# Second perceptron projection as seven half-size products per quarter of the inner width

## The reference

```
hm = rms_norm(x, norm_mlp) @ mlp_w1
x  = x + square(relu(hm)) @ mlp_w2
```

## Time and profile before

| | |
|---|---|
| device time, median of 3 runs | 1789.66 us (1789.11 to 1792.14) |
| profiled execution: span from first to last instruction | 1786.1 us |
| PE busy | 1751.6 us, 98% of the span, 9182 matmuls |
| POOL busy | 1101.4 us, 62% |
| DVE busy | 935.4 us, 52% |
| ACT busy | 474.9 us, 27% |
| chain that ended last | PE 91%, DVE 6% |

### The profile page before, as it was taken

One profiled execution on the slowest core, in us unless ns is written; L12 is line 12 of the kernel. 1 busy time (PEld: TensorE's weight loads), 2 busy tenths in 40 slices (PEclk: granted clock), 3 DMA queues, 4 the chain that ended last, 5 costly groups with the idle time before them and its releaser, 6 DMA issues.

```text
span 1786.1 us, 26166 instructions
## 1 busy us (share of the span) xinstructions
PE 1751.6 (98%) x9182; PEld 1466.1 (82%) x9182; DVE 935.4 (52%) x1537; ACT 474.9 (27%) x963; POOL 1101.4 (62%) x844
## 2 busy tenths in 40 slices
PE   6999999999999999999999999998999999999998
PEld 4888888888988888888888778886788778888887
DVE  4754727465455455554553698797466463213311
ACT  4121221211222223222321226644442522002200
POOL 3657555689754545554447658975055688667863
PEclk9999999999999999999999999999999999999999
DMA  9523222285423223322323332201032333333331
GB/s 353 175 86 95 76 82 76 83 323 165 141 85 87 76 68 93 91 78 67 90 77 95 95 88 59 72 18 43 1 118 59 90 99 98 102 94 94 94 101 52
DMA packets 282163, 176.00 MB, mean 99 GB/s; under 512 B 6064, under 2 KB 272624, under 8 KB 280816
## 3 DMA queue, kind: packets, MB, share of 16 engines
q1 hardware_dynamic: 275024, 151.01, 28.7%
q10 hardware_dynamic: 7072, 24.07, 3.7%
HBM read 172.31 MB, written 2.62 MB: 98 GB/s over the span
## 4 chain that ended last, share of the span: by engine, by line
PE 91%; DVE 6%; SPq 1%; DMA 1%; ACT 0%; issue 0%; ACTq 0%; DVEq 0%
PE acc L405 14%; PE acc L407 14%; PE acc L406 14%; PE ob L405 4%; PE ob L407 4%; PE ob L406 4%; PE acc L435 3%; PE acc L437 3%; PE acc L436 3%; PE sc L1710 2%; PE acc L453 2%; PE acc L454 2%; PE acc L455 2%; SPq L713 1%; PE sc L1615 1%; PE ob L1722 1%
## 5 line engine op out<-in xcount | busy, mean ns | idle before, releaser
L805 POOL TENSOR_TENSOR wl<-raw,wh 128x512 fp32r<-128x512 f32 x456 | 639.3, 1422 | 19.3
L802 POOL TENSOR_SCALAR wh<-raw 128x1024 fp32r<-128x1024 f32 (+1 forms) x232 | 272.6, 1175 | 567.3 <-PE acc L407 138.3
L405 PE MATMUL acc<-hh,wh 128*128 128x512 f32 x800 | 325.0, 406 | 1.4 <-ACT sq L1485 1.2
L407 PE MATMUL acc<-hh,wl 128*128 128x512 f32 x800 | 313.3, 392 | 0.0
L406 PE MATMUL acc<-hl,wh 128*128 128x512 f32 x800 | 312.7, 391 | 0.0
L405 PEld LDWEIGHTS acc<-hh,wh 128*128 128x128 f32 x800 | 151.1, 189 | 35.7 <-issue 2.7
L407 PEld LDWEIGHTS acc<-hh,wl 128*128 128x128 f32 x800 | 150.7, 188 | 32.8
L406 PEld LDWEIGHTS acc<-hl,wh 128*128 128x128 f32 x800 | 151.1, 189 | 32.1 <-issue 2.4
L405 PE MATMUL ob<-Yh,wh 128*128 128x512 f32 x256 | 100.6, 393 | 0.0
L407 PE MATMUL ob<-Yh,wl 128*128 128x512 f32 x256 | 99.8, 390 | 0.0
L406 PE MATMUL ob<-Yl,wh 128*128 128x512 f32 x256 | 99.7, 390 | 0.0
(11 more groups left out here) (575 smaller groups left out, 3706.3 us busy)
## 6 DMA issues: line engine op xcount, KB each, us to landing
raw<-in_att_w_in SPq DMA_DIRECT2D x64, 512.0 KB, 3.9
raw<-in_mlp_w SPq DMA_DIRECT2D x64, 512.0 KB, 3.8
raw<-in_ret_w_in SPq DMA_DIRECT2D x48, 512.0 KB, 3.7
ada_w<-in_ada_w ACTq DMA_DIRECT2D x8, 1536.0 KB, 7.2
raw<-in_w_in SPq DMA_DIRECT2D x23, 512.0 KB, 3.6
ada_w<-in_ada_w SPq DMA_DIRECT2D x16, 512.0 KB, 9.1
raw<-in_ret_w_out SPq DMA_DIRECT2D x16, 512.0 KB, 4.1
raw<-in_att_w_out SPq DMA_DIRECT2D x16, 512.0 KB, 4.0
```

The source lines that it names most:

```text
L405: e.matmul(bank[:, :], wh[:, s, k, :], rhs_high(k), start=(start and k == 0), stop=False)
L407: last = e.matmul(bank[:, :], wl[:, s, k, :], rhs_high(k), start=False, stop=(stop and k == k1 - 1))
L802: e.tensor_scalar(wh[:, s, 0:k1, :], raw[:, s, 0:k1, :], 1.0, 1.0, ALU.mult, ALU.mult).then_inc(high_done, 1)
L805: low = e.tensor_tensor(wl[:, s, k0:k0 + KT // 2, :], raw[:, s, k0:k0 + KT // 2, :], wh[:, s, k0:k0 + KT // 2, :].bitcast(F32), ALU.subtract)
```

## The change

W2's part of the perceptron is done by quarters of the inner width instead of halves: for each quarter 8 units of W1 and then, in place of 16 output half-tiles, one 512 x 1024 by 1024 x 1024 product by Winograd's form of Strassen's method. The activations of the quarter are a 2 x 2 arrangement A11, A12, A21, A22 (256 tokens by 512 inner features each), the weights B11, B12, B21, B22 (512 x 512 each). Seven products of half the size in each dimension replace eight: A11 B11, S1 T1, S2 T2, A22 T4, S4 B22, S3 T3, A12 B21, with sums S1 to S4 of activation blocks and T1 to T4 of weight blocks. Products are accumulated in three PSUM chains of two banks (U, V, W), and read out into x at places given in `READS`.

The output is now by tokens: the stationary operand is a 128 x 128 block of the activations, the moving one 512 columns of weights. So x itself is turned to tokens during the first quarter (`tokens_turned`, `token_out`), the norm is a per-partition scalar (`fneg` for the negative reads), no scale tile is spread, and the turning at the end is gone. The last product is done token tile by token tile, and eight DMAs of 256 KB write the result.

Who does what: POOL splits the W1 units as before and makes the weight sums T (`block_sum`, two subtractions of 128 x 512 for each of two halves of four sums); the high parts of all W2 operands are ACT copies of 128 x 1024 (`weights_high`) and their low parts DVE subtractions of 128 x 1024 (`weights_low`), 14 of each a quarter. For the activations DVE squares (`squared`), makes the sums (`combos`) and the low parts (`combos_low`), and ACT relu and the high parts (`combos_high`). W2 is loaded in blocks of 1 MB.

```diff
+OPERANDS = {"A11": 0, "S3": 1, "A12": 2, "A22": 3, "S1": 4, "S2": 5, "S4": 6}
+
+
+PRODUCT = [("A11", "B11", "U", True), ("S1", "B11", "V", True), ("S2", "B11", "U", False), ("A22", "B11", "W", True),
+           ("S4", "B22", "V", False), ("S3", "B12", "U", False), ("A12", "B21", "W", True)]
+READS = [[("U", 0, 0, 1)], [("V", 1, 1, 1)], [("U", 0, 1, 1)], [("W", 1, 0, -1)],
+         [("V", 0, 1, 1)], [("U", 1, 0, 1), ("U", 1, 1, 1)], [("W", 0, 0, 1)]]
+
+
+SUMS = [("T1", "B11", "B12", "B11"), ("T2", "B11", "B22", "B11"), ("T4", "B11", "B11", "B21"), ("T3", "B12", "B22", "B12")]
+SUM_OF = {1: "T1", 2: "T2", 3: "T4", 5: "T3"}
+BLOCKS = {"B11": 0, "B12": 1, "B21": 2, "B22": 3}
+PER = IN_UNITS + 2 * PRODUCTS
...
+        ych = at("mlp_high", [P, 7, 4, 2 * P], 0, F32R)
+        ycl = at("mlp_low", [P, 7, 4, 2 * P], 28 * KB, F32R)
+        blocks = at("mlp_blocks", [P, 4, 4, S], 56 * KB)
+        ykeep = at("mlp_kept", [P, 4, 3, 2 * P], 96 * KB)
+        ygroup = [at("mlp_group0", [P, 5, 2 * P], 88 * KB), sb("mlp_group1", [P, 5, 2 * P])]
...
+        CHAIN = {"U": ob, "V": sc, "W": [st, bc]}
...
+        def slot_used(m):
+
+            if m < 0:
+                return unit_used, total_units + m + 1
+            q, r = divmod(m, PER)
+            if r < IN_UNITS:
+                return PE.at(f"fi{q}{r}")
+            return PE.at(f"fp{q}{(r - IN_UNITS) // 2}{(r - IN_UNITS) % 2}")
+
+        def in_slot(q, j):
+            return (PER * q + j) % RING
+
+        def product_slot(q, i, h):
+            return (PER * q + IN_UNITS + 2 * i + h) % RING
...
+            load_in(0, range(RING))
+            load_in(0, (4, 5))
+            e.wait_ge(*V.at("nfss"))
+            load_block(0, "B11")
+            load_in(0, (6, 7))
+            load_block(0, "B12")
+            load_in(1, range(RING))
+            load_block(0, "B22")
+            load_block(0, "B21")
+            for q in range(1, QUARTERS):
+                e.wait_ge(*V.at(f"w_lo{q - 1}31"))
+                load_block(q, "B11")
+                e.wait_ge(*V.at(f"w_lo{q - 1}41"))
+                e.wait_ge(*G.at(f"T3{q - 1}1"))
+                load_block(q, "B22")
+                e.wait_ge(*V.at(f"w_lo{q - 1}51"))
+                load_block(q, "B12")
+                e.wait_ge(*V.at(f"w_lo{q - 1}61"))
+                load_block(q, "B21")
+                load_in(q, range(RING, IN_UNITS))
+                if q + 1 < QUARTERS:
+                    load_in(q + 1, range(RING))
...
+            def split_in(q, j):
+                n, s = q * IN_UNITS + j, in_slot(q, j)
+                x = raw[:, n % RING, :, :]
+                e.wait_ge(raw_full[n % RING], (total_units + n) // RING * 16 + 16)
+                e.wait_ge(*slot_used(PER * q + j - RING))
+                e.tensor_scalar(wh[:, s, :, :], x, 1.0, 1.0, ALU.mult, ALU.mult).then_inc(*G.done(f"f_hi{q}{j}"))
+                e.wait_ge(*G.at(f"f_hi{q}{j}"))
+                for k0 in (0, KT // 2):
+                    low = e.tensor_tensor(wl[:, s, k0:k0 + KT // 2, :], x[:, k0:k0 + KT // 2, :],
+                                          wh[:, s, k0:k0 + KT // 2, :].bitcast(F32), ALU.subtract)
+                low.then_inc(*G.done(f"f_lo{q}{j}"))
+
+            def block_sum(q, name, dst, a, b, h):
+                before = {"T1": 0, "T2": 1, "T4": 2}
+                if name in before:
+                    e.wait_ge(*V.at(f"w_lo{q}{before[name]}{h}"))
+                for x in (a, b):
+                    e.wait_ge(block_in[x], 16 * q + 16)
+                e.wait_ge(*G.last())
+                for c in range(2):
+                    o, x, y = (block_half(n, h)[:, c * S:(c + 1) * S] for n in (dst, a, b))
+                    last = e.tensor_tensor(o, x, y, ALU.subtract)
+                last.then_inc(*G.done(f"{name}{q}{h}"))
+
+            for q in range(QUARTERS):
+                for j in range(IN_UNITS):
+                    split_in(q, j)
+                for name, dst, a, b in SUMS:
+                    for h in range(2):
+                        block_sum(q, name, dst, a, b, h)
...
+            def token_out(k):
+                e.wait_ge(*PE.at(f"x_turned{k}"))
+                e.activation(xT[:, k, :], ob[k % 2][:, :], ACT.Copy).then_inc(*AC.done(f"x_tokens{k}"))
+
+            def relu(q, j):
+                e.wait_ge(*PE.at(f"fi{q}{j}"))
+                if q or j >= 6:
+                    e.wait_ge(*V.at(f"y_lo{q if j >= 6 else q - 1}{j + 4 if j < 4 else j + 2 if j < 6 else j - 2}"))
+                e.activation(y_pair(j), acc[j % 2][:, :].rearrange("p (a n) -> p a n", a=2), ACT.Relu)\
+                 .then_inc(*AC.done(f"y_relu{q}{j}"))
+
+            def combos_high(q, j):
+                e.wait_ge(*V.at(f"y_sum{q}{j}"))
+                src, dst = ((ykeep[:, j, 0:2, :], ych[:, 0:2, j, :]) if j < 4 else
+                            (ygroup[j % 2][:, :, :], ych[:, 2:7, j - 4, :]))
+                e.activation(dst, src, ACT.Copy).then_inc(*AC.done(f"y_hi{q}{j}"))
+
+            def weights_high(q, i, h):
+                of = PRODUCT[i][1]
+                e.wait_ge(*(G.at(f"{SUM_OF[i]}{q}{h}") if i in SUM_OF else (block_in[of], 16 * q + 16)))
+                e.wait_ge(*slot_used(PER * q + IN_UNITS + 2 * i + h - RING))
+                e.activation(flat(wh[:, product_slot(q, i, h), :, :]), block_half(of, h), ACT.Copy)\
+                 .then_inc(*AC.done(f"w_hi{q}{i}{h}"))
+
+            for q in range(QUARTERS):
+                for j in range(IN_UNITS):
+                    if q == 0:
+                        token_out(j)
+                    relu(q, j)
+                    combos_high(q, j)
+                    if j >= 4:
+                        weights_high(q, (j - 4) // 2, (j - 4) % 2)
+                for i in range(PRODUCTS - 2):
+                    for h in range(2):
+                        weights_high(q, i + 2, h)
...
+            def tokens_turned(k):
+                e.wait_ge(*AC.at(f"nfsq{k}"))
                 if k >= 2:
...
+            def product_free(q, i):
+                chain = PRODUCT[i][2]
+                before = [n for n in range(i) if PRODUCT[n][2] == chain]
+                if before or q:
+                    n = before[-1] if before else max(n for n in range(PRODUCTS) if PRODUCT[n][2] == chain)
+                    return V.at(f"x_read{q if before else q - 1}{n}")
+                return {"U": AC.at(f"x_tokens{KT - 1}"), "V": V.at("nfroot"), "W": V.at("nfroot")}[chain]
+
+            def product_block(q, i, k, t):
+                of, _, chain, start = PRODUCT[i]
+                s, c = product_slot(q, i, k // 2), OPERANDS[of]
+                high, low = (x[:, c, k, t * P:(t + 1) * P] for x in (ych, ycl))
+                bank, n = CHAIN[chain][t][:, :], 4 * (k % 2)
+                w, v = flat(wh[:, s, n:n + 4, :]), flat(wl[:, s, n:n + 4, :])
+                e.matmul(bank, high, w, start=(start and k == 0), stop=False, skip_group_check=True)
+                e.matmul(bank, low, w, start=False, stop=False, skip_group_check=True)
+                return e.matmul(bank, high, v, start=False, stop=(k == 3), skip_group_check=True)
+
+            def product_quarter(q, i):
+                e.wait_ge(*product_free(q, i))
+                by_token = q == QUARTERS - 1 and i == PRODUCTS - 1
+                for h in range(2):
+                    e.wait_ge(*V.at(f"w_lo{q}{i}{h}"))
+                    if by_token:
+                        continue
+                    for k in (2 * h, 2 * h + 1):
+                        if i == 0:
+                            e.wait_ge(*V.at(f"y_lo{q}{k}"))
+                        if i == 1:
+                            e.wait_ge(*V.at(f"y_lo{q}{4 + k}"))
+                        for t in range(2):
+                            last = product_block(q, i, k, t)
+                    last.then_inc(*PE.done(f"fp{q}{i}{h}"))
+                if by_token:
+                    for t in range(2):
+                        for k in range(4):
+                            last = product_block(q, i, k, t)
+                        last.then_inc(*PE.done(f"last{t}"))
...
+                    if q == 0 and j:
+                        if j == 2:
+                            e.wait_ge(*V.at("nfss"))
+                            columns(e, dg, 0, "first", "last", "nfcols")
+                        tokens_turned(j - 1)
+                        if j == IN_UNITS - 1:
+                            tokens_turned(j)
+                for i in range(PRODUCTS):
+                    product_quarter(q, i)
...
+            def squared(q, j):
+                o = y_pair(j)
+                e.wait_ge(*AC.at(f"y_relu{q}{j}"))
+                e.tensor_tensor(o, o, o, ALU.mult).then_inc(*V.done(f"y_raw{q}{j}"))
+
+            def combos(q, j):
+                e.wait_ge(*V.at(f"y_raw{q}{j}"))
+                if j < 4:
+                    e.tensor_tensor(ykeep[:, j, 1, :], ykeep[:, j, 0, :], ykeep[:, j, 2, :], ALU.subtract)\
```

(89 more changed lines are left out.)

144 lines of the change are left out of this document (36 added, 108 removed).

## The result

The changed kernel takes 1826.53 us (median of 4 runs, 1822.95 to 1826.63) against 1790.89 us before on the same chip: a ratio of 1.0199, 95% interval 1.0182 to 1.0216. It is slower by some 36 us. The forecast was 1828.

A forecast was written before the change was run, and what follows sets the result against it. PE's matmul starts, 0.227 us apart, were taken to bound the perceptron. Span 1786.1 less 24.4 won plus 63.1 of stalls gave 1824.8, plus 3.6 to the median 1828 us; range 1804 to 1843, its own 1817 to 1838.

The forecast's parts named there:

- What is removed: Perceptron and its end: four units less (21.8 us), spread norm gone, shorter end, slightly dearer turning; 24.4 us won.
- The turning: First quarter: PE waits for ACT's token copies and relu in units 2 to 7 and before product 0; 17.5 us.
- The ladder: Last W1 unit to product 2: chain of waits across ACT, DVE, POOL; 7.0 us a quarter, 5.2 in the first.
- the port: DVE instructions with two SBUF inputs and POOL's wait for each other; 5.0 us in three quarters, 3.0 in the first.
- nine meetings at 0.335: DVE and POOL meeting at their shared port in the ladder, about nine instructions at a mean 0.335 us each.
- upper bound of 9.4 us a quarter: Most the port could cost: 15 instructions a quarter at 0.63 us; the exclusive-lock rule would put the sum toward it.
- The clock: Rival: the clock falls while PE idles 5 to 8 us; 1860 us and more, chance 0.04.
- 0.2 to start again: PE after a wait: 0.2 us to restart, added to the waits in the turning and before product 2.
- The step from span to median: Whole kernel: the runs' median lies 3.6 us over the profiled span, taking 1824.8 to 1828 us.
- The faster rival: Product 2 isn't late, ladder under 10.9 us, only the turning's stalls remain; 1783 us, chance 0.11.

The follow-up runs named there:

- e9_square_from_psum: e8_early_weights with VectorE's square reading x from PSUM as second operand, the bank freed by it instead of by relu: 1770.57 us, 0.991 of the kernel before.
- e3_relu_first: Changed kernel with ScalarE's relu ahead of the token copies and turned tiles in the banks of chain V instead of U: 1816.59 us.
- e1_no_sums: Changed kernel without GpSimd's weight sums T1 to T4, every product taking the plain block (output not the reference's): 1790.85 us.
- e2_scratch_sums: Changed kernel with the weight sums still made but written to an unread scratch tile, products taking plain blocks: 1809.2 us.
- the fillers: Changed kernel with unused 512-column matmuls put ahead of TensorE's known waits: 1819.14 us.
- e5_streams: e3_relu_first plus A12 B21 second, A22 T4 last; on VectorE sums ahead of low parts, additions between weight parts: 1784.33 us, 0.9976 of the kernel before.
- e8_early_weights: e5_streams with the four weight parts of products 0 and 1 one unit earlier on ScalarE and VectorE: 1775.09 us, 0.9924 of the kernel before.

## Why the prediction was right, step by step

*What is removed.* Four units, 21.8 us: PE has 9082 matmuls instead of 9182 (96 of the products, 4 of the spread norm), and the spacing in the products is 0.227 us where the clock is full. The end: last matmul at 1817.35, end of the span 1821.1, 3.8 us as forecast, against 5.9. From the first perceptron matmul to the end of the span, the kernel before takes 1786.1 - 1425.4 = 360.7 us and e9_square_from_psum, which has almost no waits, 1767.6 - 1425.1 = 342.5. So 18.2 of the 24.4 us to be won are really won there; of the other 6.2, 4.9 are the waits that are left and about 1 the starts after them. The 24.4 us were there; what they took back is the rest of this section.

*The turning.* Forecast 17.5 us. In the trace product 0 starts 64.1 us after the first matmul, where 47.5 are work (eight units, turning and columns): 16.6 us late, 14.5 of them waits. The reading was right in place and kind. At 1434.90 ACT copies a token tile, 1435.39 it does the relu that had been ready, and PE goes on at 1436.13:

```profile
1434.27 0.60 PE L2489 MATMUL ob<-const,xT 128*128 128x128 f32 x4
1436.13 0.47 PE L2478 MATMUL acc<-hh,wh 128*128 128x512 f32 x1 [1.27 <-ACT mlp_kept L1570]
```

e3_relu_first then shows what I had not put in the sum: with these waits gone, 4.4 us come back before product 1. There VectorE's weight part for it starts at 1485.45, takes 1.22 and is ready at 1486.67, and PE goes on at 1486.77, while ScalarE's last token copy was done at 1482.28. The waits had covered that rung too.

*The ladder.* This is the main term. Forecast: product 2 starts 12.4 us late in three quarters and 8.4 in the first. Measured: product 0 of the second quarter at 1579.47, product 2 at 1600.71, 21.2 us where 10.9 are work: 10.3 late, the same in the other two, and 7.4 in the first (1487.47 to 1505.71). Together 38.4 against 45.6. The rungs, from ACT's, DVE's and POOL's timelines:

```profile
1581.89 0.58 ACT L1570 ACTIVATE mlp_group<-acc 128x512 f32<-128x512 f32 x1
...
1596.44 1.06 ACT L1583 ACTIVATE wh<-mlp_blocks 128x1024 fp32r<-128x1024 f32 x1 [3.66 <-POOL mlp_blocks L965]
```
```profile
1582.50 1.54 DVE L3381 TENSOR_TENSOR mlp_group<-mlp_group 128x512 f32<-128x512 f32 x1 [1.63 <-ACT mlp_group L1570]
1583.96 1.48 DVE L3397 TENSOR_TENSOR mlp_low<-mlp_group,mlp_high 128x1280 fp32r<-128x1280 f32 x1
1585.37 0.41 DVE L3390 TENSOR_TENSOR mlp_group<-mlp_kept,mlp_group 128x256 f32<-128x256 f32 x1
1585.81 0.42 DVE L3391 TENSOR_TENSOR mlp_group<-mlp_group,mlp_kept 128x256 f32<-128x256 f32 x1
...
1588.03 2.53 DVE L3397 TENSOR_TENSOR mlp_low<-mlp_group,mlp_high 128x1280 fp32r<-128x1280 f32 x1 [0.20 <-ACT mlp_high L1577]
1590.49 3.55 DVE L3403 TENSOR_TENSOR wl<-mlp_blocks,wh 128x1024 fp32r<-128x1024 f32 x2
1597.53 1.41 DVE L3403 TENSOR_TENSOR wl<-mlp_blocks,wh 128x1024 fp32r<-128x1024 f32 x1 [3.50 <-ACT wh L1583]
1599.05 1.61 DVE L3419 SCALAR_TENSOR_TENSOR xT<-ob,rs,xT 128x512 f32<-128x512 f32 x2
```
```profile
1592.86 3.56 POOL L965 TENSOR_TENSOR mlp_blocks<-mlp_blocks 128x512 f32<-128x512 f32 x2 [1.16 <-DVE wl L3403]
```

Each rung is where it was put, but the sizes were not. Relu 7 starts 2.4 us after product 0. The forecast has the same 2.4 (0.25 and 2.2 late) without the port, and 2.0 more for six meetings at the port in a turn of the cycle, together 4.4. In e1_no_sums relu 7 starts 1.6 us after product 0 (1578.33 and 1576.75). So the cycle alone was 0.8 us too long in the sum, and GpSimd's sums add 0.8 to it and not 2.0. From relu 7 on, dependent sums on DVE start 0.03 us after one another (1585.37 + 0.41 to 1585.81); I had taken 0.15 from an instruction with PSUM operands. And the meetings at the port in this ladder are 1.54 - 0.69 = 0.85 for the squares, 2.53 - 1.49 = 1.0 for the low parts, 3.55 - 2.35 = 1.2 for the two weight parts, 3.56 - 2.54 = 1.0 for T2, 0.2 for the last weight part: 4.3 us where nine meetings at 0.335 had been put at 3.0. With the 0.8 of the cycle the port comes to 5.1 us, against 5.0 in the sum. That this total fits is luck: five meetings at 0.86 on average in the ladder, not nine at 0.335. The 17.6 us between e1_no_sums and e2_scratch_sums fit the forecast's 18.0 for the port in the same way. Of the 2.1 us by which the ladder was too long in each of three quarters, 0.8 are the cycle, 0.4 the dependent sums and 0.6 the starts after waits, which don't delay product 2's start; 0.3 stay open.

What a meeting costs is the rest of the other engine's instruction. Low parts 7 start at 1588.03, beside a subtraction of GpSimd's that started first; GpSimd's next one runs until 1591.69, and VectorE's weight part ends 1.09 us behind it, at 1592.78:

```profile
1587.91 1.31 POOL L965 TENSOR_TENSOR mlp_blocks<-mlp_blocks 128x512 f32<-128x512 f32 x1 [4.42 <-DVE wl L3403]
1589.16 2.53 POOL L965 TENSOR_TENSOR mlp_blocks<-mlp_blocks 128x512 f32<-128x512 f32 x1
```
```profile
1590.49 2.29 DVE L3403 TENSOR_TENSOR wl<-mlp_blocks,wh 128x1024 fp32r<-128x1024 f32 x1
```

The Trainium skill, SBUF — State Buffer, "SBUF: two separate sides", states that a VectorE instruction with two SBUF inputs and a GpSimd instruction that reads SBUF lock the shared pair of ports against each other, for the whole instruction of the one that starts first. The traces agree: these three lines, and the square in e9_square_from_psum, 688 ns with one SBUF input where the means with two were 890 and 1225. The forecast had read from this rule that the sum would lie toward its upper bound of 9.4 us a quarter. It did not (5.1), because fewer instructions met than the fifteen counted, not because a meeting was cheap.

*The clock.* Here the forecast failed. I gave it as a rival with a chance of 0.04 and 1860 us, all or nothing, and the sum has nothing for it. It fell in every quarter, in short pieces, 65 slow matmuls. The step that was wrong is "0.2 to start again": after a wait the trace has 0.1 us more where the clock holds (0.34 to the next start, as at 1592.83) and 0.4 more where it is half (0.6 at 1600.71), followed by 5 to 13 slow matmuls. Behind product 2 this came to 3.0, 1.7, 2.6 and 1.5 us in the four quarters, 8.8 us, of which the fillers took away 8.4.

*The total.* Turning 16.6, ladder 38.4 and clock 8.8 make 63.8 us of stalls against 63.1 in the sum. The ladder was 7 us too long in the sum and the clock 9 us too cheap, so that the total agrees is in good part luck. From the first perceptron matmul to the end of the span the forecast has 360.7 - 24.4 + 63.1 = 399.4 us and the trace 397.7. The step from span to median was off as well. Each execution of the changed kernel lies 1.8 us above its own span, where the sum put 3.6. The profiled one, with a span of 1821.1, was the shortest of four. The others have spans of 1824.7 to 1824.8 and a mean granted clock of 0.983 to 0.984 instead of 0.986, so the trace shows the cost of the clock at its least.

*The faster rival.* Product 2 would have had to be ready within 10.9 us. It was not, but e5_streams and e8_early_weights show what its condition was: not faster instructions but another order of the same ones. I had priced it only as an error in my durations.

## What to carry to other kernels

Trading matmuls for work on other engines has two tests. The first is the share of each engine, which passed here (60%). The second is the longest chain of waits across engines within the time that the remaining matmuls cover, and it failed: 21 us against 11. Write that ladder down rung by rung before building, and look for rungs that stand there only because of the order in a stream; moving them (e8_early_weights) was worth 51 us out of 394 with no operation removed. Count also what PE loses behind a wait: the slow matmuls cost 9 us on top of the waits. Give a VectorE instruction a PSUM operand where it has two SBUF ones and GpSimd is busy.
